# One kernel, five norms: the first job behind a norm multiplies activations that are not yet divided by their root

## The reference

```python
def rms_norm(x, gain):
    x32 = x.astype(jnp.float32)
    y = x32 * lax.rsqrt(jnp.mean(x32 * x32, axis=-1, keepdims=True) + EPS)
    return (y * gain.astype(jnp.float32)).astype(x.dtype)
...
    mod = c_act @ w_ada[l] + b_ada[l]
    sh1, sc1, g1, sh2, sc2, g2 = [m[:, None, :] for m in jnp.split(mod, 6, axis=-1)]
    h = rms_norm(x, norm1_g[l]) * (1.0 + sc1) + sh1
    x = x + g1 * mixer_sublayer(h, ...)          # its first product is h @ w_in[l]
    h2 = rms_norm(x, norm2_g[l]) * (1.0 + sc2) + sh2
    gate, up = jnp.split(h2 @ w_ffn_in[l], 2, axis=-1)
    x = x + g2 * ((jax.nn.silu(gate) * up) @ w_ffn_out[l])
```

## Time and profile before

| | before |
|---|---|
| median of the timed runs | 3044.2 us |
| profiled execution, its own time | 3045.66 us |
| its span, first to last instruction | 3043.9 us |
| TensorE busy | 2848.7 us, 94% |
| VectorE busy | 1400.2 us, 46% |
| ScalarE busy | 1103.0 us, 36% |
| GpSimd busy | 232.2 us, 8% |
| mean granted clock of TensorE | 0.975 |
| TensorE's share of the chain that ended last | 84% |

### The profile page before, as it was taken

How to read it: one execution, slowest core, us unless ns; L and a number is a source line. 1 busy time by engine, 2 the same in 40 slices (tenths; PEclk the granted TensorE clock), 3 DMA queues, 4 the chain that set the end, 5 groups by cost and what they waited for, 6 DMA issues and landing times.

```text
span 3043.9 us, 36720 instructions
## 1 busy us (share of the span) xinstructions
PE 2848.7 (94%) x15602; PEld 2249.3 (74%) x15602; DVE 1400.2 (46%) x1791; ACT 1103.0 (36%) x1339; POOL 232.2 (8%) x203
## 2 busy tenths in 40 slices
PE   6998989999989899999989999989899999899998
PEld 4875867887867677677778878777675777688876
DVE  5474555443455554345554443445443244533322
ACT  4374233222144432435432221344324454332222
POOL 1011311000020100011010000010100100100001
PEclk9998999999999999999999999999999999999999
DMA  8430014433331132122233433321231211322221
GB/s 317 153 145 15 4 46 156 152 138 118 131 111 56 49 123 110 65 106 88 91 133 139 150 136 137 104 73 56 80 118 42 86 56 44 123 81 99 94 87 56
DMA packets 46943, 309.68 MB, mean 102 GB/s; under 512 B 5531, under 2 KB 6427, under 8 KB 13500
## 3 DMA queue, kind: packets, MB, share of 16 engines
q1 hardware_dynamic: 44684, 297.33, 27.1%
q0 software_dynamic: 2096, 10.00, 0.9%
HBM read 302.58 MB, written 4.72 MB: 101 GB/s over the span
## 4 chain that ended last, share of the span: by engine, by line
PE 84%; ACT 7%; DVE 5%; issue 2%; DMA 1%; SPq 0%; ACTq 0%; POOL 0%; DVEq 0%
PE bank L2045 64%; PE bank L1985 5%; PE bank L2335 3%; PE bank L2145 2%; PE bank L2034 2%; PE bank L2355 2%; ACT WH L893 1%; DMA raw<-in_wstream_dram 1%; PE bank L2479 1%; PE bank L2346 1%; PE bank L2474 1%; ACT L958 1%; DVE WL L1399 1%; PE bank L2371 1%; PE bank L2107 0%
## 5 line engine op out<-in xcount | busy, mean ns | idle before, releaser
L2045 PE MATMUL bank<-HH,WH 128*128 128x512 f32 x2304 | 932.5, 405 | 61.5 <-DVE HL L1475 47.8
L2045 PE MATMUL bank<-HL,WH 128*128 128x512 f32 x2304 | 908.4, 394 | 0.0
L2045 PE MATMUL bank<-HH,WL 128*128 128x512 f32 x2304 | 907.5, 394 | 0.0
L1399 DVE TENSOR_TENSOR WL<-raw,WH 128x2048 fp32r<-128x2048 f32 (+2 forms) x263 | 490.7, 1866 | 708.7 <-ACT WH L893 707.6
L2045 PEld LDWEIGHTS bank<-HH,WH 128*128 128x128 f32 x2304 | 438.3, 190 | 181.5 <-issue 71.6
L893 ACT ACTIVATE WH<-raw 128x2048 fp32r<-128x2048 f32 (+3 forms) x223 | 395.7, 1775 | 411.5 <-PE bank L2045 396.6
L2045 PEld LDWEIGHTS bank<-HL,WH 128*128 128x128 f32 x2304 | 437.8, 190 | 95.9 <-issue 6.5
L2045 PEld LDWEIGHTS bank<-HH,WL 128*128 128x128 f32 x2304 | 437.2, 190 | 96.2
L2045 PE MATMUL bank<-AH,WH 128*128 128x512 f32 x492 | 195.2, 397 | 8.6 <-DVE AL L1519 8.6
L2045 PE MATMUL bank<-AL,WH 128*128 128x512 f32 x492 | 194.8, 396 | 0.0
L2045 PE MATMUL bank<-AH,WL 128*128 128x512 f32 x492 | 194.8, 396 | 0.0
(11 more groups left out here) (345 smaller groups left out, 3303.9 us busy)
## 6 DMA issues: line engine op xcount, KB each, us to landing
raw<-in_wstream_dram SPq DMA_DIRECT2D x256, 1024.0 KB, 4.8
raw<-in_wstream_dram SPq DMA_DIRECT2D x24, 512.0 KB, 3.5
raw<-in_wstream_dram SPq DMA_DIRECT2D x12, 768.0 KB, 4.2
bgam<-in_consts_dram POOLq DMA_DIRECT2D x2, 1792.0 KB, 7.0
bias_dram<-bias_row POOLq DMA_DIRECT2D x8, 320.0 KB, 6.6
xT<-in_x_dram SPq DMA_DIRECT2D x2, 1024.0 KB, 8.4
toep<-bias_dram POOLq DMA_DIRECT2D x8, 256.0 KB, 3.4
out_dram<-ost SPq DMA_DIRECT2D x4, 512.0 KB, 2.7
```

The lines of the kernel that those rows point to most:

```text
L1399: TT(WL[:, wi % 2, now], raw[:, j.load % RAW, now], WH[:, wi % 2, now].bitcast(F32), ALU.subtract).then_inc(s["w_split"], 2 if half is Non ...
L2045: last = MM(o[m][0:cw, :], a, b, start=j.first and u == 0 and q == 0, stop=j.last and u == j.units - 1 and q == 2)
```

## The change

Behind norms 1 to 5 the first job (`gate` or `aqf`, called `FIRST`) no longer multiplies the finished activations. It multiplies U = x * `acol`, again as a high and a low part. ScalarE makes the high part directly behind each square and VectorE the low part, mostly while the last jobs in front of the norm run. They lie in new tiles `UH` and `UL` for norms 1, 3 and 5, and in `HH` and `HL` themselves for norms 2 and 4.

TensorE multiplies the shift with the job's weights first: 32 matmuls with 2 columns (`mod2` holds the shift's high and low part). Then it does units 0 and 1, then the sums of the squares, then units 2 to 7. VectorE multiplies the job's two banks by `nr` (`post`), and ScalarE adds the bias inside the SiLU or the sigmoid. The scaled tiles `HH` and `HL` are still made, now for the second job. `post` stands in VectorE's steps behind the low part of the fifth tile; in norms 2 and 4 a tile of `HH` is overwritten only when the first job has used it (`f_used`).

The ada step behind the last `wout` or `down` job in front of a norm now stands in front of that job.

```diff
--- before.py
+++ after.py
@@ -58,6 +58,9 @@
...
+LAST_OUT = (("wout", 3), ("down", 11))
...
     def job(kind, layer, i, every=2):
+        whole = kind != "down" or i % 3 == 2
+        chunk = whole and (kind == "down" or sum(x[0] == "job" for x in steps + [("job",)]) % every == 0)
+        if chunk and (kind, i) in LAST_OUT:
+            ada_chunk()
         steps.append(("job", kind, layer, i))
-
-        whole = kind != "down" or i % 3 == 2
-        if whole and (kind == "down" or sum(x[0] == "job" for x in steps) % every == 0):
+        if chunk and (kind, i) not in LAST_OUT:
             ada_chunk()
...
         SG = arena("SG", 88, [2, S])
+        UH = arena("UH", 0, [KD, S], F32R)
+        UL = arena("UL", 16, [KD, S], F32R)
+        mod2 = arena("mod2", 94, [KD, 2], F32R)
+        bpart = arena("bpart", 94.125, [2, 2])
+        mbias = arena("mbias", 94.25, [2, 2])
...
+
+        FIRST = {m: r_ for r_, m in EARLY.items()}
+
+        def unscaled(r):
+
+            return (UH, UL) if r % 2 else (HH, HL)
+
+        def all_read(r):
+
+            return next(JOBS[m].w for m, x in enumerate(STEPS) if x[:2] == ("job", "down") and x[2] == ffns(r) - 1
+                        and x[3] == 0) if r % 2 == 0 else JOBS[STEPS.index(("job", "wout", r // 2, 0))].w
...
             def squares(r, tiles):
+                for k in tiles:
+                    square(r, k)
+                    if 0 < r < FINAL:
+                        if k == 0:
+                            layer, g = NORM_MOD[r]
+                            act.wait_ge(s["n_acol"], r + 1 + (r >= DOUBLE))
+                            act.wait_ge(s["n_bias_ps"], r - 1)
+                            A(mod2[:, :, 0], mod[:, layer, g, :], ACT.Copy).then_inc(s["n_mod"], 1)
+                            act.wait_ge(s["gemm_done"], all_read(r))
+                        act.wait_ge(s["dve_evac"], tile_count(r, k))
+                        A(unscaled(r)[0][:, k, :], xT[:, k, :], ACT.Identity, scale=acol[:, k:k + 1]
+                          ).then_inc(s["n_uhigh"], 1)
+
+            def square(r, k):
                 if r == DOUBLE:
                     return
-                for k in tiles:
...
                 if r:
                     rstd(r)
+                if r in EARLY:
+                    act.wait_ge(s["n_bias_ps"], r)
+                    if r > 1:
+                        act.wait_ge(s["n_bias"], 2 * r - 2)
+                    A(bpart[:, :, :], bank[5][:, 0:4].rearrange("p (m x) -> p m x", m=2), ACT.Copy
+                      ).then_inc(s["n_bias_cp"], 1)
...
                     for k in range(KD):
+                        if r and r % 2 == 0:
+                            if k < KD - 1:
+                                act.wait_ge(s["f_used"], 7 * (r // 2 - 1) + k + 1)
+                            else:
+                                act.wait_ge(s["gemm_done"], gemm_before(n) + 1)
...
+                if n in FIRST:
+                    r = FIRST[n]
+                    act.wait_ge(s["n_bias"], 2 * r)
+                    act.wait_ge(s["n_post"], 2 * r)
+                    b, nb = mbias[:, 0, :], mbias[:, 1, :]
+                    if kind == "gate":
+                        for m in range(2):
+                            A(SG[:, m, :], SG[:, m, :], ACT.Silu, bias=b[:, m:m + 1]).then_inc(s["act_evac"], 1)
+                    else:
+                        a = aslot[0]
+                        A(a["q"][:, :], a["q"][:, :], ACT.Silu, bias=b[:, 0:1]).then_inc(s["act_evac"], 1)
+                        A(a["KK"][:, 0, :], a["G1"][:, 1, :], ACT.Sigmoid, scale=-1.0, bias=nb[:, 1:2]
+                          ).then_inc(s["act_evac"], 1)
+                        A(a["G1"][:, 1, :], a["G1"][:, 1, :], ACT.Sigmoid, bias=b[:, 1:2]).then_inc(s["act_evac"], 1)
+                    return
...
                     dve.wait_ge(s["dve_evac"], mod_ready_count(layer, g + 1))
+                    if r > 1:
+                        dve.wait_ge(s["n_scaled"], 8 * r)
...
                     dve.wait_ge(s["n_acol"], r + 1 + (r >= DOUBLE))
...
+            def unscaled_low(r, tiles):
+
+                layer, g = NORM_MOD[r]
+                H, L = unscaled(r)
+                for k in tiles:
+                    dve.wait_ge(s["n_uhigh"], 8 * (r - 1) + k + 1)
+                    STT(L[:, k, :], xT[:, k, :], acol[:, k:k + 1], H[:, k, :].bitcast(F32), ALU.mult, ALU.subtract
+                        ).then_inc(s["n_ulow"], 1)
+                    if k == 0:
+                        dve.wait_ge(s["n_mod"], 2 * r - 1)
+                        TT(mod2[:, :, 1], mod[:, layer, g, :], mod2[:, :, 0].bitcast(F32), ALU.subtract
+                           ).then_inc(s["n_mod"], 1)
+
+            def post(n, r):
+
+                f = JOBS[EARLY[r]]
+                dve.wait_ge(s["gemm_done"], f.w + 1)
+                dve.wait_ge(s["n_bias_cp"], r)
+                TT(mbias[:, 0, :], bpart[:, :, 0], bpart[:, :, 1], ALU.add).then_inc(s["n_bias"], 1)
+                dve.wait_ge(s["n_bias"], 2 * r - 1)
+                TS(mbias[:, 1, :], mbias[:, 0, :], -1.0, None, ALU.mult).then_inc(s["n_bias"], 1)
+                if f.kind == "aqf" and heads_done(n):
+                    dve.wait_ge(s["mixed"], heads_done(n))
+                for m in range(2):
+                    t = SG[:, m, :] if f.kind == "gate" else aslot[0]["G1"][:, 1, :] if m else aslot[0]["q"][:, :]
+                    TT(t, bank[2 * (f.bank % 2) + m][:, :], nr[:, :], ALU.mult).then_inc(s["n_post"], 1)
+
+            def norm(n, r):
+                if NORM_MOD[r]:
+                    layer, g = NORM_MOD[r]
+                if r == 0:
+                    columns(0)
                 if r == DOUBLE:
                     squares(LATE[r])
                 if r in EARLY:
+                    unscaled_low(r, LATE[r])
                     split(JOBS[EARLY[r]].w + 1)
                 dve.wait_ge(s["n_rstd"], r + 1)
...
+                    if k == 5 and r in EARLY:
+                        post(n, r)
...
-                elif st[0] == "square" and st[1] == DOUBLE:
-                    squares(range(2 * st[2], 2 * st[2] + 2))
+                elif st[0] == "square":
+                    tiles = range(2 * st[2], 2 * st[2] + 2)
+                    if st[1] < FINAL and st[2] == 0:
+                        columns(st[1])
+                    if st[1] == DOUBLE:
+                        squares(tiles)
+                    if st[1] < FINAL:
+                        unscaled_low(st[1], tiles)
...
+                elif n in FIRST:
+                    X = unscaled(FIRST[n])
...
+                if n in FIRST:
+                    r = FIRST[n]
+                    if heads_done(n):
+                        pe.wait_ge(s["h_low"], heads_done(n))
+                    pe.wait_ge(s["n_mod"], 2 * r)
+                    if r > 1:
+                        pe.wait_ge(s["n_bias_cp"], r - 1)
+                    for m in range(2):
+                        for u in range(j.units):
+                            wh, wl = (x[:, sl, u * wd + P * m:u * wd + P * m + P] for x in (WH, WL))
+                            for q, w in enumerate((wh, wl)):
+                                last = MM(bank[5][:, 2 * m:2 * m + 2], w, mod2[:, u, :], start=u == 0 and q == 0,
+                                          stop=u == j.units - 1 and q == 1)
+                    last.then_inc(s["n_bias_ps"], 1)
                 for u in range(j.units * now[0] // PARTS, j.units * (now[-1] + 1) // PARTS):
+                    if n in FIRST:
+                        if u == 2:
+                            squares(n, FIRST[n])
+                        pe.wait_ge(s["n_ulow"], 8 * (FIRST[n] - 1) + u + 1)
                     if first_use:
                         pe.wait_ge(s[first_use[0]], first_use[1] + u + 1)
                     for m in range(2 if wd == CW else 1):
@@ -2044,6 +2170,8 @@
                         for q, (a, b) in enumerate(((wh, xh), (wh, xl), (wl, xh))):
                             last = MM(o[m][0:cw, :], a, b, start=j.first and u == 0 and q == 0,
                                       stop=j.last and u == j.units - 1 and q == 2)
+                    if n in FIRST and FIRST[n] % 2 == 0 and u < j.units - 1:
+                        last.then_inc(s["f_used"], 1)
                 if now[-1] == PARTS - 1:
                     last.then_inc(s["gemm_done"], 1)
...
                 if st[0] == "norm":
-                    if nxt is not None:
-                        FIRST_USE[nxt] = ("n_low", 8 * r)
+                    if r == 0:
+                        FIRST_USE[nxt] = ("n_low", 0)
+                    elif nxt is not None:
+                        FIRST_USE[next(m for m in range(nxt + 1, len(STEPS)) if STEPS[m][0] == "job")] = ("n_low", 8 * r)
...
                 elif st[0] == "norm":
-                    if nrm:
+                    if nrm == FINAL:
                         squares(n, nrm)
```

(6 more changed lines are left out.)

2 lines of the change are left out of this document (1 added, 1 removed).

## The result

The changed kernel takes 3058.6 us (median of 5, 3054.8 to 3063.7) against 3044.2 us (median of 5, 3043.8 to 3046.9): the ratio is 1.0044, 95% interval 1.0029 to 1.0059. It is slower by more than a measurement can miss, where 3037.3 us was predicted. The profiled execution took 3059.0 us, its span is 3057.2 us, 13.3 us more than before.

A forecast was written before the change was run, and what follows sets the result against it. TensorE, busy 94% of the span, was taken as the bound, so only its waits or work count. Third-job gains of 14.4 us less 7.2 (clock) and 0.3 (norm 1) made 6.9 us: 3037.3 against 3044.2 us, range 3027 to 3048.

The forecast's parts named there:

- Small matmuls: Ahead of the first job on TensorE: 32 two-column matmuls per norm at 0.0925 us each, 3.0 us.
- the forecast up to the third job: From the preceding job's end to the third job's start: gains of 14.4 us in sum over five norms.
- the slower rival: Small matmuls don't keep TensorE's clock up, so first units and sums run slow: 15.6 us slower, 3060 us; chance 0.14.
- The clock: Behind the third job's new waits TensorE runs at 1.2 GHz for a stretch: 7.2 us lost together.
- my 2.6: Norms 2 and 4: slow clock behind a wait of 5.2 us or more costs 2.6 us each, 5.2 us.
- 1.3 at even odds: Norms 1, 3 and 5: slow clock behind 3.3 us waits costs 1.3 us at even odds, 2.0 us for three.
- no second stall: Rival: the third job's weights come in time in all five norms, giving 3007 us; chance 0.05.
- The 0.3 us at norm 1: Work in front of norm 1, where two ada steps stand close together: costed at 0.3 us.
- norm 2's 37.6: Norm 2 before the change: 37.6 us from the preceding job's end to the third job, including the ada step's wait.

The follow-up runs named there:

- Run 5: Changed kernel with 4 small matmuls and 13 unread 512-column matmuls in place of the 32 small ones in each of five norms: 3049.2 us, ratio 1.0011.
- run 3: Changed kernel with the third job's weights made earlier, behind the fifth HH tile and the last HL tile: 3029.1 us, ratio 0.9943.
- run 9: Changed kernel with the change in norms 1, 3 and 5 only, moved ada steps kept: 3048.2 us, ratio 1.0009.
- run 10: Changed kernel with the change in norms 2 and 4 only, moved ada steps kept: 3052.5 us, ratio 1.0026.
- run 12: Changed kernel without its moved ada steps: 3054.3 us, ratio 1.0030.
- run 2: Changed kernel with all 32 small matmuls behind the first job and the copy of their sums behind the fifth HH tile: 3035.4 us, ratio 0.9971.
- run 4: Changed kernel with the small matmuls behind the first job and the third job's weights made early: 3023.5 us, ratio 0.9932.
- run 1: Changed kernel with 4 small matmuls instead of 32 in each of five norms, results not the reference's: 3033.7 us, ratio 0.9967.
- run 7: Changed kernel with 28 of the 32 small matmuls left out and the third job's weights early, results not the reference's: 3003.9 us, ratio 0.9860.
- run 8: Changed kernel with small matmuls spread 5 or 6 behind each third to eighth unit of the first job, third job's weights early: 3018.5 us, ratio 0.9905.
- run 13: Changed kernel with small matmuls spread behind units of the first job, third job's weights where the change put them: 3032.8 us, ratio 0.9960.
- run 14: Changed kernel with spread small matmuls and early third-job weights, but the ada step in its old place: 3019.5 us, ratio 0.9909.
- run 11: Kernel before the change with only the ada step moved ahead of the last wout and down job: 3041.2 us, ratio 0.9983.

## Why the prediction was wrong

The mechanism of the stages was right: the wait for `HL` went, a wait for `WL` came to the third job, in the sizes named. Two steps failed, and together they are 19.5 us of the 21.3 us of error. The rest is small: 0.3 us from the third jobs of norms 2 and 4 read 0.16 us late, 0.5 us at norm 1 (T came 0.8 us later, not 0.3), and 1.1 us because the profiled execution lay 1.46 us above the median before and 0.4 us above it now.

*"Small matmuls", taken at 0.0925 us each and at full clock: 13.8 us.* The table is 13.9 us above the forecast up to the third job. Their own price, 3.46 us for 32 instead of 3.0, makes 2.3 us, and 0.3 more at norm 1; a run at 1.2 GHz inside them 1.7 us (4.67 and 3.98 less twice 3.46); the first units 8.4 us (22.0 for what I took at 13.6); the slower `WL` of norm 2 1.1 us. Sum 13.8. The mean of four records hid the price that two of them show; I had named their 0.11 us and not used it. In the kernel before, the line behind the first of the earlier trace rows is

```profile
159.34 0.39 PE L2414 MATMUL bank<-dcol,blockones 128*128 128x32 f32 x2
```

and this second pair takes 0.22 us up to 159.56, 0.11 us each; only the first pair is quicker (0.15 us), and the record of its first weight load begins at 158.97, beside the full matmul ahead of it. The same trace has 576 steps between matmuls with 128 weight and 128 moving columns, with a median of 0.112 us. The Trainium skill (TensorE: Matmul & The Clock Gate, LDWEIGHTS), which I set aside for these records, puts a load at its columns divided by 1.2, in ns, an estimate of 107 ns for 128 columns. The trace agrees: 0.111 us from one small matmul to the next. That was the smaller error.

The larger was the sentence that excused the slower rival: "the array is never without an instruction". Run 5 shows that this does not keep the clock up: 13 full-width matmuls hold it in five of five norms, 32 two-column ones in about the same time lose it in four of five. Over the kernels with 32 ahead of the first job (the changed one, runs 3, 9, 10 and 12) it fell in 15 of 20 norms (first units of 3.8 us or more, against 2.9 or less), with all 32 behind the first job (runs 2 and 4) in six of ten, with 64 ahead in five of five, with four (runs 1 and 7) in none of ten, and spread between full matmuls in none of fifteen (runs 8, 13 and 14). Why it held in the other five of the twenty stays open. That rival, with 3052 to 3060 us, got a chance of 0.14, and in kind it was what happened. That its time came so near is partly luck: it had 13.0 us for units and sums and 7.5 us for the run itself, where 8.4 us (units) and 1.7 us were measured, and it left out the dearer small matmuls and most of what the next step cost.

*"The clock", 7.2 us for the new waits: 12.9 us measured behind the third jobs.* The drop right behind the waits of norms 2 and 4 was 1.8 and 2.0 us (13.32 and 13.54 less 11.52), less than my 2.6. But the stretches of the odd norms lost 2.0, 2.9 and 3.3 us instead of 1.3 at even odds. In norms 1 and 5, 960 matmuls take 219.55 us, not 217.91 as in norm 3, from a dip behind the 2.8 us wait; the rest sits in the 492 matmuls behind a wait for `AL`, 116.57 to 117.80 us where norms 3 and 5 had 115.04 before (norm 1 had 116.37). Run 3 removes the third job's wait and two of the stretches are back at 343.9 us; so does run 4. But runs 7 and 8 have no such wait either and still show 116.6 to 117.7 in places. Why the clock falls behind one wait for `AL` and not another of the same length stays open.

*What held.* The late weights were forecast as waits; what I did not see is that a mere change of order cures them (29.5 us, run 3): I took ScalarE's order as given, and gave the case "no second stall" 0.05 as a thing that would happen by itself. The 0.3 us at norm 1 can't be told: T of norm 1 lies between 471.2 and 475.1 in the profiles of all kernels, edited there or not. And the ada step's 3.6 us (run 11) belonged to norm 2's 37.6: I noticed it, and still counted norm 2's gain as the new first job's. Norm 2's `WL` of 3.37 us, 1.1 us of that norm's 8.3, I had at 2.29.

## What to carry over

Price a tiny matmul by one with as many weight columns, however few columns it streams (here 0.111 us, half of a full one), and by what a run of them does to the clock of what follows. In this kernel they were cheapest between full-width ones, behind the sums that a chain waits for, and dearest in a run ahead of them. When a first stall is cured by more work on a helper engine, look at that engine's order for the weights of the job after next, and move that copy ahead of the work that nobody needs yet. Of two cures, test each alone and both together: here the causes added within what the runs can tell, while one cure (the later place) already held part of the other's gain.

## What was unexpected of the hardware

- Matmuls with 128 weight columns and 2 moving ones start 0.111 us apart at 2.4 GHz and 0.213 us apart at 1.2 GHz; the mean of 0.0925 us over the four records in the earlier trace rows was not the price.
- TensorE's clock fell from 2.4 to 1.2 GHz while it did 2-column matmuls back to back without idle time (854.17 in norm 2), and not while it did 512-column ones for about the same time (run 5).
- VectorE's subtraction of two 128x2048 tiles took 2.29 us in all 103 places of the 16 profiles where it began ahead of the GpSimd addition that it overlapped, and 2.5 to 3.4 us (mostly 3.37) in 94 of the 97 where an addition was already under way. In the kernel before, the one at 885.95 behind norm 2 was of the first kind; in the changed kernel, the one at 888.23 of the second, 0.05 us behind the start of an addition.
